# Rotary half turns of layer 2: from permutation matmuls on TensorE to signed multiplies on VectorE

## The chip, the core and the metric

The kernel runs on one core of one Trainium2 chip. A core has TensorE (PE in the profile; PEld is its loading of weights), VectorE (DVE), ScalarE (ACT) and GpSimd (POOL), each with an instruction queue of its own, worked off in order, and SyncE (SP), which issues DMAs. On-chip memory is SBUF (128 partitions) and PSUM, eight banks into which TensorE writes. Engines wait for each other by semaphores. The metric is the device time of one execution in microseconds (us).

## The reference, cut to what matters

Two transformer layers run one after the other over 256 tokens of width 1024, all in float32. The first has block attention (MoBA), a linear recurrence (RWKV) and a mixture of small experts (PEER). The second has sparse attention (NSA) and latent attention (MLA) side by side, and a gated feed-forward. The change concerns the rotary embedding of the second layer alone:

```python
def rope(x, pos):
    dim = x.shape[-1]
    half = dim // 2
    inv = ROPE_THETA_2 ** (-jnp.arange(half, dtype=jnp.float32) * 2.0 / dim)
    ang = pos[:, None] * inv[None, :]
    cos = jnp.cos(ang)[None, :, None, :]
    sin = jnp.sin(ang)[None, :, None, :]
    xf = x.astype(jnp.float32)
    x1, x2 = xf[..., :half], xf[..., half:]
    return jnp.concatenate([x1 * cos - x2 * sin, x1 * sin + x2 * cos], axis=-1).astype(x.dtype)
```

NSA rotates 14 head rows of width 128: eight queries, two keys for selection, two for the window (all normalised first) and two that are compressed later (not normalised). MLA rotates parts of width 64: one key part that all heads share, and eight query parts, which lie two to a row tile.

## The kernel before, in words

**Layout.** Activations lie transposed: features on the 128 partitions, the 256 tokens along the free axis. The scratch of a layer is one tensor, `arena`, so the trace calls most operands `arena`. `F2` in it holds 22 row tiles of 128x256: rows 0 to 11 are the normalised NSA heads, 12 and 13 the compressed ones, 16 to 20 the latents of MLA, 21 its shared key part. A rotation needs x*cos + turn(x)*sin, where turn swaps the two halves of a head across partitions and negates one of them.

**The projection `w_in2`.** Its 37 weight tiles (128 output features each) are loaded through a ring of six slots (`wring`). The first 32 are multiplied in split precision: ScalarE casts a tile to its upper part (`whi`, three slots, line 490), another engine subtracts that from the tile to get the lower part (`wlo`, line 495, `tile_lo`), and TensorE makes three matmuls for each of eight blocks (lines 501 to 503). The cast of tile k waits until TensorE is done with tile k-3, the subtraction waits for the cast, and TensorE waits for the subtraction before it starts a tile. The subtraction of tiles 13 to 31 is GpSimd's (`lo_phase` in the GpSimd block); before that it is VectorE's. The last five tiles (line 531) need no split.

**The norms and turns between the tiles.** TensorE's program has small pieces between the tiles, at places fixed by numbers: after tile 13 the sums of squares (line 2437), after tile 15 the norm factors given back to all partitions (line 2457), after tile 18 the turn `pe_nsa_turn` (line 2468: seven matmuls with the permutation `rot_nsa`, 128x512 columns each, into five banks), after tile 24 the sums for MLA's latents (`pe_rank_sums`, line 2445). VectorE runs `dve_nsa` beside it: squares (lines 2355, 2357), normalising multiplies that read PSUM (line 2364), the seven multiplies of the turned rows, read from PSUM, by the sine (line 2369), the cosine product (line 2373), the squares of the latents (line 2375, which waits until tile 20 has been copied out), the sum of both rotary parts (line 2377), the blocks for compression (line 2384), and the scaling of the latents (lines 2390, 2393), which releases MLA.

**MLA's up-projections and the attention.** `dve_mla` turns the shared key after the matmul of line 2697, which TensorE's list has behind the second key tile. The attention then runs 24 NSA jobs and eight MLA jobs in a pipeline of turns (`att_pe`, `att_dve`, `att_act`, `att_pool`). Of a job, TensorE makes scores, VectorE the maximum (line 832), ScalarE the exponential, VectorE the reciprocal (lines 847, 848), GpSimd the scaling of the probabilities (line 873, two instructions), TensorE the transposes (line 757) and the product with the values. Weight matmuls left over from the projection (line 2754) fill in between. At turns 4 and 7 TensorE makes the two matmuls of MLA's query turn (line 2703), and at turns 6, 8, 10 and 12 VectorE does the four steps of `turn_queries` (lines 2613 to 2620).

Of the kernel before, what the change touches and what calls it, by code (L numbers as in the profile page):

```python
# [12 lines left out]
ALU = mybir.AluOpType  # L13
# [89 lines left out]
CONST2 = [("rot_nsa", 128), ("rot_mla", 128), ("sum_all", 128), ("sum_rope", 64), ("give_all", 512),  # L103
# [17 lines left out]
def shape_constants():  # L121
# [31 lines left out]
    def table(width):  # L153
        half = width // 2
        inv = (np.float32(10000.0) ** (-np.arange(half, dtype=np.float32) * np.float32(2.0) / np.float32(width)))
        ang = np.arange(S, dtype=np.float32)[None, :] * inv.astype(np.float32)[:, None]
        ang = np.tile(ang, (128 // half, 1))
        return [np.cos(ang), np.sin(ang)]
# [3 lines left out]
    two = [rotation(128, 64), rotation(64, 32), sum_all, sum_rope, give_all,  # L162
# [27 lines left out]
def build_layer_pair(nc, a):  # L190

    with ExitStack() as ctx:
# [2077 lines left out]
        def pe_w_in2(pe):  # L2270
            first, ring0 = FIRST["w_in2"], RING0["w_in2"]

            for t in range(2, RAW2):
                pe.wait_ge(lo_ready, nth_split[first + t])
                if t >= 2 + BANKS:
                    pe.wait_ge(ring_free, ring0 + t - BANKS + 1)
                raw8(pe, bank[(ring0 + t) % BANKS], first + t).then_inc(tile_done, 1)
            pe.wait_ge(x_lo, XLO[3])
            ring_tiles_split(pe, "w_in2", RAW2, SUMS_AT)
            pe_nsa_sums(pe)  # L2280
            ring_tiles_split(pe, "w_in2", SUMS_AT, GIVE_AT)
            pe_nsa_give(pe)
            ring_tiles_split(pe, "w_in2", GIVE_AT, ROT_AT)
            pe_nsa_turn(pe)
            ring_tiles_split(pe, "w_in2", ROT_AT, RANK_AT)
            pe_rank_sums(pe)
            ring_tiles_split(pe, "w_in2", RANK_AT, SPLIT2)
            pe.wait_ge(xn_ready, 3 * KT)
            for k in range(SPLIT2, COUNT["w_in2"]):
                n, r = first + k, ring0 + k  # L2290
                pe.wait_ge(landed[n % SLOTS], count_at(n))
                pe.wait_ge(ring_free, r - BANKS + 1)
                matmul8_tokens(pe, bank[r % BANKS], n % SLOTS).then_inc(tile_done, 1)

        SUMS_AT, GIVE_AT, ROT_AT, RANK_AT = 14, 16, 19, 25
# [45 lines left out]
        n_qn, n_q = sem("n_qn"), sem("n_q")  # L2341
# [10 lines left out]
        def dve_nsa(dve, v):  # L2352
# [109 lines left out]

        def pe_nsa_turn(pe):
            pe.wait_ge(n_qn, 6)
            for g in range(7):
                if g >= 5:
                    pe.wait_ge(n_q, g - 4)
                pe.matmul(bank[3 + g % 5][:, :], c2["rot_nsa"], r2["F2"][:, 512 * g:512 * g + 512], start=True,
                          stop=True).then_inc(head_rot, 1)
# [87 lines left out]
        TURN_AHEAD = (4, 7)  # L2557
# [5 lines left out]
        def dve_mla(dve, v):  # L2563
# [8 lines left out]
            dve.wait_ge(head_rot, 9)  # L2572
            v.then(dve.tensor_tensor(ro[:, 4, :], bank[5][:, 0:S], c2["mla_sin"], ALU.mult))
# [36 lines left out]
            def turn_queries(step):  # L2610
                if step < 2:
                    dve.wait_ge(head_rot, 9 + step + 1)
                    dve.tensor_tensor(ro[:, 2 * step:2 * step + 2, :], two(2), over(c2["mla_sin"], 2), ALU.mult)\
                       .then_inc(n_q, 1)
                elif step == 2:
                    v.did(dve.tensor_tensor(qb[:, 8:12, :], qb[:, 8:12, :], over(c2["mla_cos"], 4), ALU.mult))
                elif step == 3:
                    dve.wait_ge(n_q, 9)
# [23 lines left out]
        def pe_mla(pe):  # L2642
# [52 lines left out]
            def turned_key():  # L2695
                pe.wait_ge(l_q, 1)
                pe.matmul(bank[5][:, 0:S], c2["rot_mla"], krr, start=True, stop=True).then_inc(head_rot, 1)

            def turned_queries(g):
                pe.wait_ge(l_q, 5)  # L2700
                if g:
                    pe.wait_ge(n_q, 8)
                pe.matmul(bank[2][:, :], c2["rot_mla"], r2["qb"][:, (8 + 2 * g) * S:(10 + 2 * g) * S],
                          start=True, stop=True).then_inc(head_rot, 1)

            for name, t in MIX:
# [4 lines left out]
                if (name, t) == ("uk", 1):  # L2711
                    turned_key()
                elif (name, t) == ("cmp_k", 5):
# [15 lines left out]
            def beside(t):  # L2729
# [5 lines left out]
                if t in TURN_AHEAD:  # L2735
                    turned_queries(TURN_AHEAD.index(t))
# [543 lines left out]
```

## Time and profile before

| what | value |
|---|---|
| device time, median of 3 runs | 1661.33 us (1660.74 to 1662.58) |
| span of the profiled execution | 1660.7 us |
| TensorE busy | 1620.8 us (98%) |
| VectorE busy | 1255.8 us (76%) |
| ScalarE busy | 823.8 us (50%) |
| GpSimd busy | 162.5 us (10%) |

The span is the time from the first to the last instruction of one execution; it is 0.6 us below the median of the timed runs. Busy time is what an engine's instructions cover together. The stretch of the projection in question lies from about 1208 us (GpSimd's first subtraction) to 1300 us (first up-projection of MLA), the attention from about 1350 us.

### The profile page before, as it was taken

How to read it: one execution, taken by the hardware profiler on the slowest of the kernel's cores; microseconds unless marked ns; L12 is line 12 of the kernel's file. 1: busy time of each engine (PE TensorE's matmuls, PEld its weight loads, DVE VectorE, ACT ScalarE, POOL GpSimd, SP SyncE). 2: the span in 40 equal slices, each digit the busy share in tenths (PEclk: the TensorE clock that was granted, in tenths of full speed). 3: DMA queues.
4: the chain of work that ended last, by engine and by line, in shares of the span. 5: the costliest groups of instructions: out<-in, count | busy, mean ns of one | idle time of the engine just before them, and what ended most of it. 6: DMA issues, size and time to landing. Idle time of an engine off the chain costs nothing.

```text
span 1660.7 us, 32559 instructions
## 1 busy us (share of the span) xinstructions
PE 1620.8 (98%) x11538; PEld 1430.8 (86%) x11538; DVE 1255.8 (76%) x2664; ACT 823.8 (50%) x1500; POOL 162.5 (10%) x134
## 2 busy tenths in 40 slices
PE   6999999999999999999999999999999999999998
PEld 4887988899988878888888888888889777999998
DVE  6885538759989988788888888888858256588887
ACT  3544111365469845555555555555744255544443
POOL 0020000017700000000000000000057014100000
PEclk9999999999999999999999999999999999999999
DMA  9742135855642288777777777777545651345553
GB/s 353 288 147 89 41 119 205 321 193 176 223 133 64 97 262 269 232 235 237 236 236 238 240 235 240 235 238 237 181 134 161 220 172 39 98 143 178 186 181 127
DMA packets 102625, 316.98 MB, mean 191 GB/s; under 512 B 11392, under 2 KB 21376, under 8 KB 102144
## 3 DMA queue, kind: packets, MB, share of 16 engines
q1 hardware_dynamic: 101664, 311.27, 56.3%
q10 hardware_dynamic: 864, 4.39, 0.7%
q8 instruction: 65, 1.06, 0.3%
q14 instruction: 32, 0.26, 0.1%
HBM read 309.71 MB, written 5.90 MB: 190 GB/s over the span
## 4 chain that ended last, share of the span: by engine, by line
PE 54%; DVE 15%; issue 14%; ACT 12%; DMA 2%; DVEq 1%; SPq 1%; POOL 0%; ACTq 0%
PE bank L501 9%; PE bank L502 9%; PE bank L503 9%; ACT whi L490 6%; DVE xn L2201 3%; PE bank L1301 3%; DVE Wlo L2184 2%; DVE arena L2190 2%; DVE wlo L495 2%; ACT arena L2031 2%; PE bank L2068 2%; PE bank L2070 2%; PE bank L2072 2%; PE bank L476 2%; PE bank L1587 2%
## 5 line engine op out<-in xcount | busy, mean ns | idle before, releaser
L490 ACT CAST whi<-wring 128x1024 fp32r<-128x1024 f32 x386 | 403.4, 1046 | 156.9 <-PE bank L503 84.7
L495 DVE TENSOR_TENSOR wlo<-wring,whi 128x1024 fp32r<-128x1024 f32 x341 | 415.3, 1223 | 52.2 <-ACT whi L490 42.8
L501 PE MATMUL bank<-xboth,whi 128*128 128x256 f32 x1032 | 296.9, 288 | 3.9 <-DVE wlo L495 2.2
L502 PE MATMUL bank<-xboth,whi 128*128 128x256 f32 x1032 | 291.9, 283 | 0.0
L503 PE MATMUL bank<-xboth,wlo 128*128 128x256 f32 x1032 | 291.9, 283 | 0.0
L501 PEld LDWEIGHTS bank<-xboth,whi 128*128 128x128 f32 x1032 | 197.8, 192 | 8.7 <-issue 3.8
L502 PEld LDWEIGHTS bank<-xboth,whi 128*128 128x128 f32 x1032 | 197.9, 192 | 0.7 <-issue 0.5
L503 PEld LDWEIGHTS bank<-xboth,wlo 128*128 128x128 f32 x1032 | 197.8, 192 | 0.0
L495 POOL TENSOR_TENSOR wlo<-wring,whi 128x1024 fp32r<-128x1024 f32 x45 | 114.9, 2560 | 811.7 <-ACT whi L490 811.6
L514 PE MATMUL bank<-xboth,whi 128*128 128x512 f32 x704 | 188.7, 390 | 0.0
L2068 PE MATMUL bank<-whi,Whi 128*128 128x512 f32 x512 | 159.7, 393 | 2.9 <-DVE Wlo L2184 2.9
L2070 PE MATMUL bank<-wlo,Whi 128*128 128x512 f32 x512 | 158.6, 391 | 0.0
L2072 PE MATMUL bank<-whi,Wlo 128*128 128x512 f32 x512 | 157.7, 389 | 0.0
L514 PEld LDWEIGHTS bank<-xboth,whi 128*128 128x128 f32 x704 | 132.5, 188 | 24.0
L2072 PEld LDWEIGHTS bank<-whi,Wlo 128*128 128x128 f32 x512 | 96.1, 188 | 21.0
L2070 PEld LDWEIGHTS bank<-wlo,Whi 128*128 128x128 f32 x512 | 96.1, 188 | 21.0
L2068 PEld LDWEIGHTS bank<-whi,Whi 128*128 128x128 f32 x512 | 95.1, 188 | 21.9 <-issue 3.1
L522 PEld LDWEIGHTS bank<-xboth,wlo 128*128 128x128 f32 x704 | 96.0, 190 | 6.9
L2139 ACT ACTIVATE arena<-arena 128x256 f32<-128x256 f32 x88 | 36.8, 418 | 128.0 <-DVE arena L2190 128.0
L522 PE MATMUL bank<-xboth,wlo 128*128 128x256 f32 x704 | 98.2, 282 | 0.0
L2193 DVE TENSOR_TENSOR arena<-arena 128x256 f32<-128x256 f32 x88 | 56.0, 636 | 52.4 <-ACT arena L2139 52.4
L2137 ACT COPY arena<-bank 128x256 f32<-128x256 f32 x88 | 32.9, 373 | 90.9 <-PE bank L514 90.9
(397 smaller groups left out, 2889.8 us busy)
## 6 DMA issues: line engine op xcount, KB each, us to landing
wring<-in_w SPq DMA_DIRECT2D x463, 512.0 KB, 3.5
arena<-in_ada SPq DMA_DIRECT2D x48, 512.0 KB, 7.4
xn<-in_ada SPq DMA_DIRECT2D x96, 256.0 KB, 2.7
h_spill<-arena SPq DMA_DIRECT2D x37, 128.0 KB, 1.7
arena<-h_spill SPq DMA_DIRECT2D x37, 128.0 KB, 3.9
wring<-in_w SPq DMA_DIRECT2D x6, 384.0 KB, 4.8
wring<-in_w SPq DMA_DIRECT2D x8, 256.0 KB, 3.3
arena<-in_const ACTq DMA_DIRECT2D x1, 1215.0 KB, 5.5
```

What stands on the lines that cost most here:

```text
L490: act.copy(whi[:, n % HSLOTS, :], wring[:, n % SLOTS, :]).then_inc(hi_ready, 1)
L495: eng.tensor_tensor(wlo[:, n % SLOTS, :], wring[:, n % SLOTS, :], whi[:, n % HSLOTS, :].bitcast(F32), ALU.subtract).then_inc(lo_ready, 1)
L501: pe.matmul(out, h, xh, start=start, stop=False, **kw)
L502: pe.matmul(out, h, xl, start=False, stop=False, **kw)
L503: return pe.matmul(out, l, xh, start=False, stop=stop, **kw)
L514: return pe.matmul(out, whi[:, n % HSLOTS, k * 128:k * 128 + 128], xboth[:, k, :, :], start=(k == 0), stop=(k == KT - 1))
L522: pe.matmul(out[:, 0:S], wlo[:, n % SLOTS, k * 128:k * 128 + 128], xhi[:, k, :], start=False, stop=False)
L1301: mm = pe.matmul(bank[r % BANKS][:, 0:S], blocks(tile % SLOTS, k), xn[:, k, :], start=(k == 0), stop=(k == KT - 1))
L2068: pe.matmul(tok_accs[b][f][:, :], Wh, h[:, f * 512:(f + 1) * 512], start=first, stop=False)
L2070: pe.matmul(tok_accs[b][f][:, :], Wh, l[:, f * 512:(f + 1) * 512], start=False, stop=False)
L2072: mm = pe.matmul(tok_accs[b][f][:, :], Wl, h[:, f * 512:(f + 1) * 512], start=False, stop=last)
L2193: dve.tensor_tensor(ge[:, b, :], ge[:, b, :], g, ALU.mult).then_inc(w_gated, 1)
```

## The change

The permutation matrices and every matmul with them go: seven in the projection, one for MLA's shared key, two for its queries. The sine table gets the sign of the turn: it holds the sine on the partitions of the first half of a head and minus the sine on those of the second. VectorE then multiplies one half's rows by the table's rows of the same half and writes the product on the partitions of the other half; both inputs of these multiplies lie in SBUF. For NSA these are two instructions on 64 partitions with 14x256 elements each, for MLA's key four on 32 partitions with 256, for its queries four on 32 partitions with 4x256, two at turn 6 and two at turn 8. They wait for the normalised rows instead of a matmul. `pe_rank_sums`, which waited until VectorE had read the turned banks, waits for the normalising multiplies.

```diff
-        return [np.cos(ang), np.sin(ang)]
+        return [np.cos(ang), np.where(p % width < half, 1.0, -1.0) * np.sin(ang)]
...
-            ring_tiles_split(pe, "w_in2", GIVE_AT, ROT_AT)
-            pe_nsa_turn(pe)
-            ring_tiles_split(pe, "w_in2", ROT_AT, RANK_AT)
+            ring_tiles_split(pe, "w_in2", GIVE_AT, RANK_AT)
...
+        thirtytwo = [slice(32 * i, 32 * i + 32) for i in range(4)]
+        nsa_swap = ((lo, hi), (hi, lo))
+        mla_swap = tuple((thirtytwo[i], thirtytwo[i ^ 1]) for i in range(4))
...
             dve.wait_ge(n_qn, 6)
-            for g in range(7):
-                dve.wait_ge(head_rot, 1 + g + 1)
-                ins = dve.tensor_tensor(ro14[:, 2 * g:2 * g + 2, :], bank[3 + g % 5][:, :].rearrange("p (m t) -> p m t", m=2),
-                                        over(c2["nsa_sin"], 2), ALU.mult)
-                ins.then_inc(n_q, 1)
-            dve.wait_ge(n_q, 7)
+            for dst, src in nsa_swap:
+                v.did(dve.tensor_tensor(ro14[dst, :, :], F2[src, 0:14, :], over(c2["nsa_sin"][src], 14), ALU.mult))
+            v.settle()
...
         def pe_rank_sums(pe):
-            pe.wait_ge(n_q, 7)
+            pe.wait_ge(n_qn, 6)
...
-            dve.wait_ge(head_rot, 9)
-            v.then(dve.tensor_tensor(ro[:, 4, :], bank[5][:, 0:S], c2["mla_sin"], ALU.mult))
+            for dst, src in mla_swap:
+                v.did(dve.tensor_tensor(ro[dst, 4, :], krr[src], c2["mla_sin"][src], ALU.mult))
+            v.settle()
...
                 if step < 2:
-                    dve.wait_ge(head_rot, 9 + step + 1)
-                    dve.tensor_tensor(ro[:, 2 * step:2 * step + 2, :], two(2), over(c2["mla_sin"], 2), ALU.mult)\
-                       .then_inc(n_q, 1)
+                    if step == 0:
+                        dve.wait_ge(l_q, 5)
+                    for dst, src in mla_swap[2 * step:2 * step + 2]:
+                        v.did(dve.tensor_tensor(ro[dst, 0:4, :], qb[src, 8:12, :], over(c2["mla_sin"][src], 4), ALU.mult))
...
-                if (name, t) == ("uk", 1):
-                    turned_key()
...
-                if t in TURN_AHEAD:
-                    turned_queries(TURN_AHEAD.index(t))
```

In the order of instructions on TensorE, at the end of the projection's tile 18 (lines 501 to 503 are the matmuls of a tile, line 2468 the turn), the kernel before has:

```order
L501 MATMUL bank<-xboth,whi 128x256
L502 MATMUL bank<-xboth,whi 128x256
L503 MATMUL bank<-xboth,wlo 128x256
L2468 MATMUL bank<-arena 128x512 x7
L501 MATMUL bank<-xboth,whi 128x256
L502 MATMUL bank<-xboth,whi 128x256
L503 MATMUL bank<-xboth,wlo 128x256
```

and the changed kernel at the same place:

```order
L501 MATMUL bank<-xboth,whi 128x256
L502 MATMUL bank<-xboth,whi 128x256
L503 MATMUL bank<-xboth,wlo 128x256
L501 MATMUL bank<-xboth,whi 128x256
L502 MATMUL bank<-xboth,whi 128x256
L503 MATMUL bank<-xboth,wlo 128x256
L501 MATMUL bank<-xboth,whi 128x256
```

The seven matmuls of the turn are gone, and the first matmul of tile 19 stands right behind the last one of tile 18.

In VectorE's order, the list of `dve_nsa` from the normalising multiplies on has before (line 2369 reads `bank`, PSUM):

```order
L2364 SCALAR_TENSOR_TENSOR arena<-arena,cols,bank 128x512 x6
L2369 TENSOR_TENSOR arena<-bank,arena 128x512 x7
L2373 TENSOR_TENSOR arena<-arena 128x3584
L2375 TENSOR_TENSOR arena<-arena 128x1280
L2377 TENSOR_TENSOR arena<-arena 128x3584
L2384 TENSOR_TENSOR arena<-arena,cols 128x16x15 x4
L2390 RECIPROCAL arena<-arena 128x512
L2393 SCALAR_TENSOR_TENSOR arena<-arena,cols 128x256 x5
L2384 TENSOR_TENSOR arena<-arena,cols 128x16x15 x4
```

and in the changed kernel:

```order
L2365 SCALAR_TENSOR_TENSOR arena<-arena,cols,bank 128x512 x6
L2369 TENSOR_TENSOR arena<-arena 64x3584 x2
L2371 TENSOR_TENSOR arena<-arena 128x3584
L2373 TENSOR_TENSOR arena<-arena 128x1280
L2375 TENSOR_TENSOR arena<-arena 128x3584
L2382 TENSOR_TENSOR arena<-arena,cols 128x16x15 x4
L2388 RECIPROCAL arena<-arena 128x512
L2391 SCALAR_TENSOR_TENSOR arena<-arena,cols 128x256 x5
L2382 TENSOR_TENSOR arena<-arena,cols 128x16x15 x4
```

In the place of seven multiplies of 512 columns that read PSUM stand two of 3584 columns on 64 partitions that read SBUF alone; the rest keeps its order, two line numbers lower.

In VectorE's order in the attention, at the first step of the query turn (line 832 is a job's maximum), before:

```order
L847 RECIPROCAL arena<-arena 128x2
L848 TENSOR_TENSOR arena<-arena 128x2
L2613 TENSOR_TENSOR arena<-bank,arena 128x512
L832 ISA arena<-bank,arena 128x128
L832 ISA arena 128x1
L832 ISA arena<-bank,arena 128x256
L832 ISA arena 128x1
L836 TENSOR_SCALAR arena<-arena 128x2
```

and in the changed kernel:

```order
L847 RECIPROCAL arena<-arena 128x2
L848 TENSOR_TENSOR arena<-arena 128x2
L2605 TENSOR_TENSOR arena<-arena 32x1024 x2
L832 ISA arena<-bank,arena 128x128
L832 ISA arena 128x1
L832 ISA arena<-bank,arena 128x256
L832 ISA arena 128x1
L836 TENSOR_SCALAR arena<-arena 128x2
```

One multiply of 512 columns from PSUM has become two of 1024 columns on 32 partitions from SBUF; the second step changes in the same way.

## Rows read from the trace of the kernel before

**Rows 1.** The page, busy time of each engine, and the granted clock by slices.

```profile
PE 1620.8 (98%) x11538; PEld 1430.8 (86%) x11538; DVE 1255.8 (76%) x2664; ACT 823.8 (50%) x1500; POOL 162.5 (10%) x134
...
PEclk9999999999999999999999999999999999999999
```

**Rows 2.** Busy time by windows: stretch us, PE, PEld, DVE, ACT, POOL, clock, DMA.

```profile
1227.70:1259.90 32.20, 32.20 (x232) 28.82 (x232) 20.98 (x15) 11.97 (x17) 20.48 (x8) 1.00 0.41 131
...
1600.00:1661.00 61.00, 56.20 (x467) 55.83 (x465) 48.47 (x88) 23.24 (x31) 0.00 (x0) 1.00 0.44 145
```

**Rows 3.** TensorE's timeline: start us, us, instructions [idle before <-releaser].

```profile
1236.46 6.17 PE L2468 MATMUL bank<-arena 128*128 128x512 f32 x14
1242.07 0.68 PE L501 MATMUL bank<-xboth,whi 128*128 128x256 f32 x1
```

**Rows 4.** The chain that ended last: start us, us, what.

```profile
1300.07 1.73 PE bank L2655 x8
...
1304.29 0.43 PE bank L2697 x2
...
1365.91 0.86 PE bank L2703 x2
```

**Rows 5.** VectorE's timeline over projection and MLA's start, columns as in rows 3.

```profile
1225.87 4.04 DVE L2364 SCALAR_TENSOR_TENSOR arena<-arena,cols,bank 128x512 f32<-128x512 f32 x6 [4.45 <-PE bank L2457]
1237.59 1.48 DVE L2369 TENSOR_TENSOR arena<-bank,arena 128x512 f32<-128x512 f32 x2 [7.68 <-PE bank L2468]
...
1243.40 3.89 DVE L2373 TENSOR_TENSOR arena<-arena 128x3584 f32<-128x3584 f32 x1
1249.83 3.52 DVE L2375 TENSOR_TENSOR arena<-arena 128x1280 f32<-128x1280 f32 x1 [2.54 <-ACT arena L2308]
1253.27 6.09 DVE L2377 TENSOR_TENSOR arena<-arena 128x3584 f32<-128x3584 f32 x1
...
1304.76 0.42 DVE L2573 TENSOR_TENSOR arena<-bank,arena 128x256 f32<-128x256 f32 x1 [21.82 <-PE bank L2697]
```

**Rows 6.** GpSimd's timeline in the projection, three windows.

```profile
1237.84 2.37 POOL L495 TENSOR_TENSOR wlo<-wring,whi 128x1024 fp32r<-128x1024 f32 x1 [0.49 <-ACT whi L490]
1246.72 5.28 POOL L495 TENSOR_TENSOR wlo<-wring,whi 128x1024 fp32r<-128x1024 f32 x2 [6.51 <-ACT whi L490]
...
1249.60 2.40 POOL L495 TENSOR_TENSOR wlo<-wring,whi 128x1024 fp32r<-128x1024 f32 x1
...
1252.47 3.13 POOL L495 TENSOR_TENSOR wlo<-wring,whi 128x1024 fp32r<-128x1024 f32 x1 [0.48 <-ACT whi L490]
```

**Rows 7.** GpSimd's line 495, whole run: duration ns min/median/max, starts.

```profile
L495 POOL TENSOR_TENSOR wlo<-wring,whi x45: 2365/2403/6029, 369.6 to 1274.8; 128x1024 fp32r<-128x1024 f32 x45
```

**Rows 8.** ScalarE's timeline in the projection.

```profile
1251.35 1.05 ACT L490 CAST whi<-wring 128x1024 fp32r<-128x1024 f32 x1 [1.56 <-PE bank L503]
...
1254.23 1.05 ACT L490 CAST whi<-wring 128x1024 fp32r<-128x1024 f32 x1 [1.56 <-PE bank L503]
```

**Rows 9.** VectorE's timeline in the attention.

```profile
1370.68 0.68 DVE L2613 TENSOR_TENSOR arena<-bank,arena 128x512 f32<-128x512 f32 x1
...
1375.18 0.68 DVE L2613 TENSOR_TENSOR arena<-bank,arena 128x512 f32<-128x512 f32 x1
...
1384.81 1.23 DVE L2620 TENSOR_TENSOR arena<-arena 128x1024 f32<-128x1024 f32 x1
```

**Rows 10.** GpSimd's timeline in the attention.

```profile
1370.86 0.84 POOL L873 TENSOR_SCALAR arena<-arena 128x128 f32<-128x128 f32 x2 [2.03 <-DVE arena L848]
...
1375.35 0.83 POOL L873 TENSOR_SCALAR arena<-arena 128x128 f32<-128x128 f32 x2 [1.68 <-DVE arena L848]
...
1384.99 1.75 POOL L873 TENSOR_SCALAR arena<-arena 128x128 f32<-128x128 f32 x2 [1.59 <-DVE arena L848]
```

**Rows 11.** TensorE's timeline in the attention, transposes of two jobs.

```profile
1372.11 0.49 PE L757 MATMUL bank<-keep,arena 128*128 128x128 f32 x3
...
1377.23 0.49 PE L757 MATMUL bank<-keep,arena 128*128 128x128 f32 x3
```

More of the change, by code:

```diff
@@ L102 @@
 SELECT1 = [("sum_pair", 64), ("give_pair", 256)]
-CONST2 = [("rot_nsa", 128), ("rot_mla", 128), ("sum_all", 128), ("sum_rope", 64), ("give_all", 512),
+CONST2 = [("sum_all", 128), ("sum_rope", 64), ("give_all", 512),
           ("nsa_cos", 256), ("nsa_sin", 256),
@@ L157, in table @@
         ang = np.tile(ang, (128 // half, 1))
-        return [np.cos(ang), np.sin(ang)]
+        return [np.cos(ang), np.where(p % width < half, 1.0, -1.0) * np.sin(ang)]
     t = np.arange(S).reshape(TT, 128).T[:, :, None]
     seen = (np.arange(NCMP) * CS + CB - 1)[None, None, :] <= t
-    two = [rotation(128, 64), rotation(64, 32), sum_all, sum_rope, give_all,
+    two = [sum_all, sum_rope, give_all,
            *table(128), *table(64), causal, np.where(seen, 0, NEG).reshape(128, -1), seen.any(-1),
@@ L2293, in pe_w_in2 @@
                 matmul8_tokens(pe, bank[r % BANKS], n % SLOTS).then_inc(tile_done, 1)
-        SUMS_AT, GIVE_AT, ROT_AT, RANK_AT = 14, 16, 19, 25
+        SUMS_AT, GIVE_AT, RANK_AT = 14, 16, 25
         raw_bank2 = lambda t: bank[5 + t] if t < 2 else ring_bank("w_in2", t)
@@ L2339, in build_layer_pair @@
         RAW_SCALED2 = RAW1 if 1 in RAWNORMS else 0
-        n_qn, n_q = sem("n_qn"), sem("n_q")
+        n_qn = sem("n_qn")
+        thirtytwo = [slice(32 * i, 32 * i + 32) for i in range(4)]
+        nsa_swap = ((lo, hi), (hi, lo))
+        mla_swap = tuple((thirtytwo[i], thirtytwo[i ^ 1]) for i in range(4))
         cm_x, cm_hs, cm_t, cm_ts, cm_o0, cm_kn, cm_kt, cm_kc, cm_rt = (sem(f"cm_{x}") for x in
@@ L2461, in pe_nsa_give @@
                     mm.then_inc(head_given, 1)
[L2463 to L2469, printed above, removed]
         def pe_compress(pe, i, name, t):
@@ L2556, in build_layer_pair @@
         TURN_QUERIES = (6, 8, 10, 12)
-        TURN_AHEAD = (4, 7)
         WO_UPPER, WO_LOWER = (11, 14, 17), (16, 19, 22)
@@ L2611, in turn_queries @@
                 if step < 2:
-                    dve.wait_ge(head_rot, 9 + step + 1)
-                    dve.tensor_tensor(ro[:, 2 * step:2 * step + 2, :], two(2), over(c2["mla_sin"], 2), ALU.mult)\
-                       .then_inc(n_q, 1)
+                    if step == 0:
+                        dve.wait_ge(l_q, 5)
+                    for dst, src in mla_swap[2 * step:2 * step + 2]:
+                        v.did(dve.tensor_tensor(ro[dst, 0:4, :], qb[src, 8:12, :], over(c2["mla_sin"][src], 4), ALU.mult))
                 elif step == 2:
+                    v.settle()
                     v.did(dve.tensor_tensor(qb[:, 8:12, :], qb[:, 8:12, :], over(c2["mla_cos"], 4), ALU.mult))
                 elif step == 3:
-                    dve.wait_ge(n_q, 9)
                     v.settle()
@@ L2693, in up @@
                 dict(uk=uk, uq=uq, uv=uv)[name](slot_of(n), bank[r % BANKS]).then_inc(tile_done, 1)
[L2695 to L2704, printed above, removed]
             for name, t in MIX:
@@ L2710, in pe_mla @@
                     pe_compress(pe, name == "cmp_v", name, t)
-                if (name, t) == ("uk", 1):
-                    turned_key()
-                elif (name, t) == ("cmp_k", 5):
+                if (name, t) == ("cmp_k", 5):
                     sums(1, 8)
```

## The prediction

> **What bounds the kernel now.** I read the page first: TensorE is busy for 98% of the span at the full granted clock [rows 1]. The windows then give the stretch of the change: from 1227.7 to 1259.9 us TensorE has no idle time at all, while GpSimd is busy for 20.5 and VectorE for 21.0 of 32.2 us [rows 2]. On this alone, work taken off TensorE would come out of the time whole. So the other engines' timelines come next, for how near each is to becoming the bound once the gap of the turn is closed. What the reader is to see there is a pair: the same subtraction takes GpSimd 2.37 us while VectorE works from PSUM, and up to 6.03 us elsewhere [rows 6, 7]; the same multiply of 3584 columns takes VectorE 3.89 us while GpSimd has nothing to subtract until 1246.72, nearly its end, and 6.09 us while GpSimd has subtractions to do [rows 5, 6]. Last, the chain of waits says which of the removed matmuls lie on the path: the one for MLA's key and those for its queries do [rows 4].
>
> **What is removed.** The seven matmuls of the projection hold back the tiles from 1236.46 to about 1242.45 (the first matmul of tile 19 starts at 1242.07 and runs on beside the last of the turn, 0.68 us) [rows 3]: 6.0 us. MLA's key takes 0.43 us, and two for its queries 0.86 us each [rows 4]; the second of them has no row here, as it repeats the first. That is 6.0 + 0.43 + 1.72 = 8.15 us of TensorE. VectorE no longer waits: it lay idle for 7.68 us before its first turned rows [rows 5], and for 21.82 us before the turned key.
>
> **What is added: first the rule of the rows.** The squares of the latents (1280 columns) began at 1249.83 and took 3.52 us; GpSimd's subtraction had begun at 1249.60 and ended at 1252.00, and the squares ended 1.35 us after that [rows 5, 6], about what 1280 columns take at the rate of 3584 in 3.89 us. The next subtraction, begun at 1252.47, ended at 1255.60 after 3.13 us instead of 2.40, and the sum of 3584 columns, begun at 1253.27, ended 3.76 us after that. So a VectorE instruction with both inputs in SBUF and a subtraction on GpSimd run one after the other, whichever came first, and in turns when both have more to do. The longest subtraction, 6.03 us [rows 7], is one that sat out those 3.7 us and then took its own 2.4. Multiplies that read one input from PSUM, as line 2369, left the subtraction beside them at 2.37 us [rows 5, 6].
>
> The Trainium skill states this in "SBUF — State Buffer", section "Who interferes with whom": a VectorE instruction with two SBUF inputs and a GpSimd instruction that reads SBUF share a read interface, and the second one to issue blocks until the first is done. The rows above agree, 3.76 us after the grant against 3.89 us alone. The rule speaks against this change, as its multiplies trade a PSUM input for an SBUF one; by a sum without it the projection would save its 6.0 us.
>
> **The projection, step by step.** The normalising multiplies end at 1229.91 [rows 5], and the first half's multiply starts at once. Two pair lengths follow from the rows: a 3584-column instruction and a subtraction together, 6.03 us [rows 7]; the squares and a subtraction, 1252.00 to 1255.60, 3.60 us [rows 6]. Casts come one tile of 2.88 us apart [rows 8], so GpSimd always finds a cast ready in what follows. Subtractions 13 to 18 are done. Then:
> - first half's multiply and subtraction 19: to 1236.0. TensorE, done with tile 18 at 1236.46, goes on without a wait.
> - second half's multiply and subtraction 20: to 1242.0. TensorE has been ready since 1239.3 and waits 2.7 us, with everything else on its queue behind the tile.
> - cosine product and subtraction 21: to 1248.0, a wait of 3.1 us.
> - squares and subtraction 22: to 1251.6, a wait of 0.7 us (tile 20's copy, which the squares need, is there by about 1246.5: the tile's end at 1244.9, a cast and a copy).
> - sum of both parts and subtraction 23: to 1257.7, a wait of 3.1 us.
>
> From there VectorE's instructions are short (240 columns, 0.25 us at the rate above), GpSimd needs about 2.65 us a tile against TensorE's 2.88, and TensorE waits no more. Before, tile 23 starts at 1242.45 + 4 x 2.88 = 1254.0, which fits the cast that its predecessor's end releases at 1254.23 [rows 8]. So the projection gets 1257.7 - 1254.0 = 3.7 us longer instead of 6.0 us shorter. Where an error could lie: handing over between two engines is counted inside the pairs; 0.05 us more or less at ten hand-overs is 0.5 us.
>
> **MLA's start.** TensorE loses 0.43 us there. VectorE gets four multiplies on 32 partitions; line 2573 with 256 columns took 0.42 us, so at most 1.7 us for one of 0.42. Its 21.82 us of idle time hide them; all of its work up to there was done at 1282.9, before TensorE began MLA at 1300.07 [rows 4, 5]. With the projection 3.7 us later on TensorE and about as much on VectorE, that cover stays. Without it, the cost would be 1.3 us.
>
> **The attention.** Steps 0 and 1 of the query turn cost VectorE one multiply from PSUM each, 0.68 us. Each becomes two of 1024 columns from SBUF, 1.23 us apiece by line 2620 [rows 9]. Behind them in VectorE's queue are the maxima of a later job; beside them GpSimd scales the probabilities that TensorE waits for. At line 2620 that pair of instructions took 1.75 us instead of 0.83 [rows 10], 0.92 us more. With two multiplies, GpSimd waits 0.92, does its first part (0.41), waits 1.07 for the second multiply (1024 columns at 3.76 us per 3584), and does the rest (0.41): 2.81 us, 1.98 more than now. TensorE's slack there is what passes between the end of the scaling and the transposes: 1371.70 to 1372.11 at the first step, 0.41 us, and 1376.18 to 1377.23, 1.05 us, at the second [rows 10, 11]. So TensorE waits about 1.6 and 0.95 us, against 1.72 us of matmuls gone: 0.8 us longer. Bounds: no collision at all, 1.72 us shorter; both scalings late without any slack, 3.96 - 1.72 = 2.2 us longer.
>
> **The sum.** 3.7 - 0.43 + 0.8 = 4.1 us, from the profiled execution's 1660.7 us to 1664.8. The median of the timed runs stands 0.6 above the span, so 1665.4 us, 0.25% slower. Behind the attention nothing changes, and the constants that the ScalarE queue loads get smaller by two matrices, at a place where nothing waits.
>
> What the trace does not show is a multiply on 64 partitions that reads one half and writes the other. The nearest row for its length is line 2373 with the same columns on 128 partitions, 3.89 us; I take that, as time here goes with columns. From below, it might leave GpSimd alone altogether (rival 1); from above, two such halves one after the other without a turn for GpSimd make 7.5 us of waiting for one subtraction, which by the same steps gives 1.1 us longer in the projection if the cosine product follows too (rival 3), and 3.4 us if it does not.
>
> **Rivals.**
> 1. *The half-row multiplies don't collide.* If 64 or 32 partitions, or the crossing of halves, go another way than rows 5 show, subtractions 19 to 21 come in time. The cosine product, now earlier and beside subtraction 21, then still collides with 22, the squares with 23, the sum with 24; by the same pairs tile 24 starts 1.0 us earlier than before. With 0.43 and 1.72 us it is 3.15 us shorter: 1658.2. For it: no such instruction has run beside GpSimd in this trace. Against it: even a multiply of 240 columns in line 2384 takes turns there.
> 2. *The matmuls come out whole, on the other side of zero.* Its place is the subtraction of tile 20: if that is ready by 1239.3, nothing of the above happens. It needs the long rows of GpSimd and VectorE to have another cause than each other, one that this change does not bring forward. Then 8.15 us go: 1653.2. For it: TensorE without a gap in the window [rows 2]. Against it: the long durations are, within 0.1 us, what the other engine had left plus what the work takes alone, at three hand-overs [rows 5 to 7].
> 3. *VectorE keeps going.* If the three long multiplies run without a turn for GpSimd, TensorE waits 7.1 us once, at tile 19, and the projection ends 1.1 us later; with the 0.43 and an attention where the same happens (GpSimd 2.2 us late at a step, 0.8 us longer): 1662.8. Against it: GpSimd came between two VectorE instructions at each chance in rows 5 and 6.
> 4. *The clock falls in TensorE's new gaps.* Four waits of 0.7 to 3.1 us within 20 us; at 1.2 instead of 2.4 GHz every microsecond of matmuls costs one more, so 3 us spent there give 1668.4. Against it: in the last 61 us TensorE idles for 4.8 us and the granted clock stays at 1.00 [rows 2].
>
> **How the numbers follow.** The forecast has a chance of 0.66; its own range is 1664.0 to 1667.0. Rival 1 has 0.12, rival 2 0.08, rival 3 0.09, rival 4 0.05. About 0.2% (3.3 us) is what a measurement can tell from no change, so 1658.0 and 1664.65 are the borders. Of the forecast's 0.66 about 0.54 lie above the upper one and 0.12 within; rival 4 adds 0.05 above. Half of rival 1 and all of rival 2 fall below the lower one, 0.14; the other half of rival 1 and rival 3 within. So faster 0.14, same 0.27, slower 0.59. The range leaves out rival 2 and most of rival 4 and takes in the rest, 1657.5 to 1668.0.
>
> **What would show it.** Right: GpSimd's subtractions 20, 21 and 23 in the new trace at about 6 us each from about 1236 on; VectorE's half-row multiplies at 3.9 us (the first) and 6.1 us (the second); TensorE waiting for GpSimd's line 495 in the projection, some 9.7 us in four waits, where it waits for nothing now; GpSimd's scaling at 2.8 us at two jobs of the attention; the new line of MLA's key not waited for. Wrong: subtractions at 2.4 us beside the half-row multiplies, or no wait on TensorE between tiles 18 and 24.

## The result, and the profile after

The changed kernel takes 1668.28 us (median of 5 runs, 1666.24 to 1669.43) against 1662.1 us for the kernel before (5 runs beside it, 1660.74 to 1662.78): a ratio of 1.0039, 95% interval 1.0028 to 1.0049, so 6.2 us slower where 4.1 us were forecast. The profiled execution's span is 1665.1 us, its own time 1666.98, which is 1.3 us below the median of the five. One timed run of all that follow, the sixth of the kernel with dummies ahead of tiles 20, 21 and 23, was a slow one (2006.77 us at a mean granted clock of 0.75) and enters no median.

The page of the changed kernel, busy time by engine and the group of GpSimd's subtractions (busy us, mean ns of one, idle before):

```profile
PE 1617.2 (97%) x11518; PEld 1430.5 (86%) x11518; DVE 1269.9 (76%) x2664; ACT 823.5 (49%) x1500; POOL 175.2 (11%) x134
...
L495 POOL TENSOR_TENSOR wlo<-wring,whi 128x1024 fp32r<-128x1024 f32 x45 | 123.7, 2755 | 807.3 <-ACT whi L490 807.3
```

TensorE has 20 matmuls (the trace has two for each of the program's ten) and 3.6 us of work less than in [rows 1]; the matmuls taken out were 8.15 us, and what runs longer in their place is shown below. GpSimd has the same 134 instructions and 12.7 us more in them. So something that GpSimd shares got dearer.

To see where, the trace is cut at three instructions that both kernels have: the first normalising multiply (1225.87 in [rows 5]), the squares of MLA's keys, and a subtraction of VectorE's behind the attention. The last two in VectorE's timeline before:

```profile
1310.37 2.29 DVE L2578 TENSOR_TENSOR arena<-arena 128x2048 f32<-128x2048 f32 x1 [4.26 <-ACT arena L2767]
...
1436.76 1.22 DVE L495 TENSOR_TENSOR wlo<-wring,whi 128x1024 fp32r<-128x1024 f32 x1 [1.11 <-ACT whi L490]
```

VectorE's timeline after (start us, us, instructions, idle before and what ended it):

```profile
1225.07 4.04 DVE L2365 SCALAR_TENSOR_TENSOR arena<-arena,cols,bank 128x512 f32<-128x512 f32 x6 [4.45 <-PE bank L2455]
1229.14 9.91 DVE L2369 TENSOR_TENSOR arena<-arena 64x3584 f32<-64x3584 f32 x2
1239.09 5.92 DVE L2371 TENSOR_TENSOR arena<-arena 128x3584 f32<-128x3584 f32 x1
1247.38 3.56 DVE L2373 TENSOR_TENSOR arena<-arena 128x1280 f32<-128x1280 f32 x1 [2.38 <-ACT arena L2306]
1250.86 6.09 DVE L2375 TENSOR_TENSOR arena<-arena 128x3584 f32<-128x3584 f32 x1
...
1285.21 1.76 DVE L2562 TENSOR_TENSOR arena<-arena 32x256 f32<-32x256 f32 x4
...
1313.68 2.29 DVE L2568 TENSOR_TENSOR arena<-arena 128x2048 f32<-128x2048 f32 x1 [25.80 <-ACT arena L2743]
...
1441.06 1.23 DVE L495 TENSOR_TENSOR wlo<-wring,whi 128x1024 fp32r<-128x1024 f32 x1 [1.11 <-ACT whi L490]
```

From the first mark to the second it is 88.61 us instead of 84.50 (projection and MLA's start, 4.11 longer), from the second to the third 127.38 instead of 126.39 (attention, 0.99 longer). Up to the first mark this execution happened to be 0.80 us ahead; up to the end hardly anything is added. These differences are used for every experiment, since the starts of the traces scatter by some 3 us (first mark from 1225.07 to 1227.83) whatever the edit.

GpSimd's timeline after, the subtractions of tiles 19 to 24:

```profile
1231.28 4.03 POOL L495 TENSOR_TENSOR wlo<-wring,whi 128x1024 fp32r<-128x1024 f32 x1 [3.73 <-ACT whi L490]
...
1235.26 6.00 POOL L495 TENSOR_TENSOR wlo<-wring,whi 128x1024 fp32r<-128x1024 f32 x1
...
1241.22 6.01 POOL L495 TENSOR_TENSOR wlo<-wring,whi 128x1024 fp32r<-128x1024 f32 x1
...
1247.20 2.39 POOL L495 TENSOR_TENSOR wlo<-wring,whi 128x1024 fp32r<-128x1024 f32 x1
...
1249.56 3.65 POOL L495 TENSOR_TENSOR wlo<-wring,whi 128x1024 fp32r<-128x1024 f32 x1
...
1253.16 6.00 POOL L495 TENSOR_TENSOR wlo<-wring,whi 128x1024 fp32r<-128x1024 f32 x1
```

The reader is to see the pairs of [rows 6, 7] again: each subtraction beside a multiply of 3584 columns lasts 6.0 us, the one beside the squares 3.65, the one alone 2.39. TensorE's waits between 1200 and 1450 us (us in total, times, longest):

```profile
PE bank L501 <- POOL wlo L495: 6.8, 3, 2.8
PE bank L757 <- POOL arena L873: 2.7, 3, 1.5
```

Before, the first did not exist there and the second was 0.4 us. TensorE's timeline at these waits:

```profile
1241.31 0.38 PE L501 MATMUL bank<-xboth,whi 128*128 128x256 f32 x1 [2.61 <-POOL wlo L495]
...
1242.47 0.41 PE L501 MATMUL bank<-xboth,whi 128*128 128x256 f32 x1
1242.68 0.41 PE L502 MATMUL bank<-xboth,whi 128*128 128x256 f32 x1
...
1247.29 0.38 PE L501 MATMUL bank<-xboth,whi 128*128 128x256 f32 x1 [1.34 <-POOL wlo L495]
...
1259.21 0.58 PE L501 MATMUL bank<-xboth,whi 128*128 128x256 f32 x1 [2.81 <-POOL wlo L495]
...
1262.76 0.28 PE L501 MATMUL bank<-xboth,whi 128*128 128x256 f32 x1
1262.88 0.28 PE L502 MATMUL bank<-xboth,whi 128*128 128x256 f32 x1
...
1263.48 0.81 PE L2443 MATMUL bank<-arena,keep 128*128 128x256 f32 x3
```

The matmuls after the first and the last wait start 0.21 us apart (1242.47, 1242.68), later again 0.12 (1262.76, 1262.88). The windows say why (stretch us, PE, PEld, DVE, ACT, POOL, then the granted clock, 1.00 being 2.4 GHz and 0.50 being 1.2 GHz):

```profile
1242.00:1244.00 2.00, 2.00 (x12) 2.00 (x11) 2.00 (x1) 0.00 (x0) 2.00 (x1) 0.50 0.00 0
1244.00:1246.00 2.00, 1.94 (x12) 1.74 (x11) 1.01 (x1) 0.00 (x0) 2.00 (x1) 0.72 0.00 0
...
1260.00:1262.00 2.00, 2.00 (x12) 2.00 (x11) 2.00 (x2) 0.00 (x0) 2.00 (x2) 0.50 0.00 0
```

So the waits also brought the low clock, twice, for some 3 us each.

### The profile page after: what moved, and what is told of

The parts are those of the page before. It is cut to its first block, busy times and chain, and to the rows that moved or that the text cites. A ratio compares the mean times of both kernels' runs of the same rounds, so it can differ in the third digit from the quotient of the medians.

```text
span 1665.1 us, 32516 instructions
## 1 busy us (share of the span) xinstructions
PE 1617.2 (97%) x11518; PEld 1430.5 (86%) x11518; DVE 1269.9 (76%) x2664; ACT 823.5 (49%) x1500; POOL 175.2 (11%) x134
## 4 chain that ended last, share of the span: by engine, by line
PE 51%; issue 15%; DVE 15%; ACT 12%; POOL 3%; DMA 2%; DVEq 1%; SPq 1%; ACTq 0%; POOLq 0%
PE bank L501 8%; PE bank L502 8%; PE bank L503 8%; ACT whi L490 6%; DVE xn L2201 3%; PE bank L1301 3%; DVE Wlo L2184 2%; DVE arena L2190 2%; DVE wlo L495 2%; POOL wlo L495 2%; ACT arena L2031 2%; PE bank L2068 2%; PE bank L2070 2%; PE bank L2072 2%; PE bank L476 2%
## 5 line engine op out<-in xcount | busy, mean ns | idle before, releaser
L495 POOL TENSOR_TENSOR wlo<-wring,whi 128x1024 fp32r<-128x1024 f32 x45 | 123.7, 2755 | 807.3 <-ACT whi L490 807.3
```

Of the source, the lines that this page charges most:

```text
L495: eng.tensor_tensor(wlo[:, n % SLOTS, :], wring[:, n % SLOTS, :], whi[:, n % HSLOTS, :].bitcast(F32), ALU.subtract).then_inc(lo_ready, 1)
```

## The experiments

Two theories to begin with. *Turns:* VectorE's multiplies with both inputs in SBUF and GpSimd's instructions run in turns, and that is the whole loss. *Clock:* a good part of it is TensorE's lower clock after the waits. With each group of runs the kernel before was timed again on the same chip, and the ratios are against those times.

**The changed kernel once more**, without an edit.

> The changed kernel once more, to fix the size of the change on one chip with the parts below. The traces so far differ by 4.4 us in span and the medians by 6.2 us. If the effect is the one seen in the trace (turn-taking on VectorE and GpSimd in the projection, 1.1 us in the attention, the lowered clock), it is 4.4 to 6.5 us slower than before; a run-to-run effect of another chip would show as under 3 us.

1668.48 us (1667.05 to 1671.53, 5 runs) against 1662.72 (21 runs): ratio 1.0035, 1.0021 to 1.0049. The waits are nearly the same (7.0 us in 3 instead of 6.8), but the clock fell only once. Its windows:

```profile
1242.00:1248.00 6.00, 3.93 (x22) 3.93 (x22) 5.77 (x1) 0.87 (x2) 6.00 (x2) 0.72 0.33 91
...
1260.00:1266.00 6.00, 4.03 (x29) 3.93 (x30) 6.00 (x3) 1.36 (x3) 6.00 (x3) 1.00 0.31 87
```

First to second mark: 87.32 us, 2.82 over before instead of 4.11. Same order and 1.29 us less, and the difference is tile 24 at full clock: here it takes 2.97 us (1261.97 to 1264.94) where it took 4.27 (1259.21 to 1263.48).

**NSA's half of the change alone, and MLA's alone**, each put into the kernel before:

```diff
-            ring_tiles_split(pe, "w_in2", GIVE_AT, ROT_AT)
-            pe_nsa_turn(pe)
-            ring_tiles_split(pe, "w_in2", ROT_AT, RANK_AT)
+            ring_tiles_split(pe, "w_in2", GIVE_AT, RANK_AT)
...
+            for dst, src in ((lo, hi), (hi, lo)):
+                v.did(dve.tensor_tensor(ro14[dst, :, :], F2[src, 0:14, :], over(c2["nsa_sin"][src], 14), ALU.mult))
```

```diff
-            dve.wait_ge(head_rot, 9)
-            v.then(dve.tensor_tensor(ro[:, 4, :], bank[5][:, 0:S], c2["mla_sin"], ALU.mult))
+            for dst, src in mla_swap:
+                v.did(dve.tensor_tensor(ro[dst, 4, :], krr[src], c2["mla_sin"][src], ALU.mult))
...
+                    for dst, src in mla_swap[2 * step:2 * step + 2]:
+                        v.did(dve.tensor_tensor(ro[dst, 0:4, :], qb[src, 8:12, :], over(c2["mla_sin"][src], 4), ALU.mult))
```

> The NSA part alone (no matmuls for the projection's turn, multiplies from SBUF there; MLA keeps its matmuls). Turn-taking: the projection gets some 4.5 us longer as in the whole change without the key's 0.43, so 4 to 6 us slower than before, with GpSimd's subtractions at 6 us. Rival (the loss comes from the MLA part, and the projection gains its matmuls): about 6 us faster than before.

> The MLA part alone (NSA keeps its matmuls). Turn-taking: minus 0.43 us for the key's matmul, minus 1.72 for the queries' two, plus about 2.7 us of TensorE waiting for GpSimd's scaling at two jobs, so 0 to 1 us slower than before. Rival (these waits lie beside other work): 2 us faster.

NSA alone: 1667.61 us, ratio 1.0033 (1.0024 to 1.0042, 11 runs). MLA alone: 1663.25 us, ratio 1.0 (0.9991 to 1.0009, 11 runs). TensorE's waits for GpSimd that are new, in the first and in the second (0.4 us of the second stood there before):

```profile
PE bank L502 <- POOL wlo L496: 6.9, 3, 2.8
```

```profile
PE bank L758 <- POOL arena L874: 2.7, 3, 1.5
```

NSA's half adds 3.23 us between the first two marks (with the key's matmul still in) and nothing in the attention (126.41); MLA's takes 0.45 there and adds 1.00 in the attention. Together 3.78, what the second trace of the changed kernel shows (2.82 + 1.00). The parts add up, and nearly all of the loss is NSA's.

**NSA's tables read from PSUM.** If turns are the cause, one input from PSUM ends them, with the same instructions on VectorE. ScalarE copies cosine and sine into bank 7 behind tile 15:

```diff
+                    act.copy(bank[7][:, :], r2["const2"][:, C2_AT["nsa_cos"]:C2_AT["nsa_cos"] + 2 * S]).then_inc(n_tab, 1)
...
-                v.did(dve.tensor_tensor(ro14[dst, :, :], F2[src, 0:14, :], over(c2["nsa_sin"][src], 14), ALU.mult))
+                v.did(dve.tensor_tensor(ro14[dst, :, :], F2[src, 0:14, :], over(nsa_tab["nsa_sin"][src], 14), ALU.mult))
```

The cosine product takes its table from there too.

> The changed kernel with NSA's cosine and sine tables copied to a PSUM bank by ScalarE, so that the two half-row multiplies and the cosine product keep their place, length and rows, but have one input in PSUM. Turn-taking on two SBUF inputs: VectorE runs them in 3.9 us each, GpSimd's subtractions 19 to 22 take 2.4 us, TensorE does not wait between tiles 18 and 25, and the projection is 6.0 us shorter than before: 1662.7 - 6.0 - 0.4 + 1.0 = about 1657.3. Rival (the crossing of halves or VectorE's longer list is what costs): as the changed kernel, 1668.

1657.67 us (8 runs, 1656.42 to 1659.55) against 1662.21: ratio 0.9975, 0.9965 to 0.9986, as expected. Its VectorE and a subtraction of GpSimd's beside it:

```profile
1230.40 7.80 DVE L2375 TENSOR_TENSOR arena<-arena,bank 64x3584 f32<-64x3584 f32 x2
1238.23 3.89 DVE L2377 TENSOR_TENSOR arena<-arena,bank 128x3584 f32<-128x3584 f32 x1
```

```profile
1235.40 2.42 POOL L495 TENSOR_TENSOR wlo<-wring,whi 128x1024 fp32r<-128x1024 f32 x1 [0.48 <-ACT whi L490]
```

and its first two marks:

```profile
1226.32 4.04 DVE L2370 SCALAR_TENSOR_TENSOR arena<-arena,cols,bank 128x512 f32<-128x512 f32 x6 [4.45 <-PE bank L2461]
...
1304.38 2.29 DVE L2574 TENSOR_TENSOR arena<-arena 128x2048 f32<-128x2048 f32 x1 [24.27 <-ACT arena L2749]
```

The two half-row multiplies take 7.80 instead of 9.91 us, the subtraction 2.42 instead of 6.00, and TensorE waits for no subtraction. From the first to the second mark it is 78.06 us, 6.44 shorter than before: the seven matmuls' 6.0 and the key's 0.43 come out whole. That one operand's place turns +4.11 into -6.44 shows the turns. It is what the Trainium skill states in "SBUF — State Buffer", section "Who interferes with whom", of two SBUF inputs, now seen in one kernel with and without the collision.

**MLA's tables read from PSUM**, in the query turn, by a copy into bank 2 at turn 2; NSA's part as in the changed kernel:

```diff
+                    act.copy(bank[2][:, :], r2["const2"][:, C2_AT["mla_cos"]:C2_AT["mla_cos"] + 2 * S]).then_inc(q_tab, 1)
...
-                        v.did(dve.tensor_tensor(ro[dst, 0:4, :], qb[src, 8:12, :], over(c2["mla_sin"][src], 4), ALU.mult))
+                        v.did(dve.tensor_tensor(ro[dst, 0:4, :], qb[src, 8:12, :], over(mla_tab["mla_sin"][src], 4), ALU.mult))
```

> The changed kernel with MLA's tables in PSUM bank 2 for the query turn alone. Turn-taking: GpSimd's scaling goes back from 2.8 to 0.8 us at the two jobs and from 1.5 to 0.6 at the third, TensorE waits less by 2.5 to 3 us, so 2.5 to 3 us faster than the changed kernel: about 1665.5. Rival (VectorE's own length, 2.4 instead of 0.7 us, delays the maxima): within 0.5 us of the changed kernel.

1668.2 us (6 runs, 1665.42 to 1668.64), ratio 1.0032 (1.002 to 1.0044): a miss. The attention got 1.5 us shorter than in the changed kernel (125.86 us), not the 2.5 to 3 expected, and in this trace the projection, with two falls of the clock at other tiles, was 0.75 us longer. Its VectorE, and its TensorE, at the first of the two pieces:

```profile
1375.46 2.45 DVE L2608 TENSOR_TENSOR arena<-arena,bank 32x1024 f32<-32x1024 f32 x2
```

```profile
1379.78 0.39 PE L760 MATMUL bank<-keep,arena 128*15 128x128 f32 x2 [0.55 <-POOL arena L873]
```

GpSimd's scaling beside the first piece is back at 0.84 us, but TensorE still waits, here 0.55 us and after the second piece 0.54. The reading, which is the rival of the expectation: the piece itself, 2.45 us, holds up the maxima behind it in VectorE's queue, and the next scaling starts late. The last experiment tests it.

**Both.** The two edits together.

> Both tables in PSUM. Turn-taking: the matmuls come out nearly whole, 8.15 us and 0.3 more at the cosine product of the queries: about 1654.3, 0.5% faster than before. Rival: what is gained in one place is lost in the other, over 1657.

1656.52 us (1655.43 to 1657.85), ratio 0.9966 (0.9952 to 0.998). The marks give -6.43 and -0.52, what the two edits gave apart. It is 2.2 us above the 1654.3 hoped for: by the marks 1.5 us of that lie in the attention, at the same waits as in the kernel before this one (0.55 and 0.55 us).

**The turn put off.** Instead of tables in PSUM, the twelve normalised heads are turned once GpSimd's last subtraction is done, from SBUF (the two that are compressed stay in place); MLA as in the last kernel:

```diff
+            dve.wait_ge(ring_free, ring0 + 14)
+            turn14(12, 14, latent_squares)
...
+            dve.wait_ge(lo_ready, nth_split[FIRST["w_in2"] + SPLIT2 - 1])
+            turn14(0, 12)
```

> The changed kernel with the turn of the 12 normalised heads moved behind GpSimd's last subtraction, into VectorE's idle time before MLA, from SBUF as it is; only the two heads for compression are turned in the projection. MLA's query tables in PSUM as in x4. Turn-taking: no subtraction is made to wait by a long multiply (only by the squares), so as x5: about 1654. Rival (length or crossing of the multiplies): also about 1654, but then x3 does not gain. If the moved 13 us of multiplies come too late for MLA, slower than x5 by what they are late.

1656.35 us (1654.35 to 1656.45), ratio 0.9961 (0.9948 to 0.9975); first to second mark -6.44, as with the tables in PSUM, and -0.20 in the attention. That is 2.3 us above the 1654 expected, but as near to the kernel with both tables (1656.52) as was expected. GpSimd's last subtraction ends at 1271.76; behind it VectorE has:

```profile
1273.13 6.74 DVE L2372 TENSOR_TENSOR arena<-arena 64x3072 f32<-64x3072 f32 x2
```

The same multiplies from SBUF cost nothing where GpSimd has nothing to do. So it is not the multiply that is dear, but its company.

**Dummy matmuls against the low clock.** Ten products with the identity (twenty matmuls in the trace, 2.40 us) each ahead of tiles 20, 21 and 24 of the changed kernel:

```diff
+            for k in (20, 21, 24):
+                pe_warm(pe, 7, 10)
+                ring_tiles_split(pe, "w_in2", k, {20: 21, 21: 24, 24: 25}[k])
```

> The changed kernel with ten matmuls of 128 columns of no use (2.15 us each time) ahead of tiles 20, 21 and 24, where TensorE waits 2.6, 1.3 and 2.8 us for GpSimd. If TensorE's gaps lower the granted clock and that costs what tile 24 took too long (4.27 us instead of 2.88), the clock stays at 1.00 from 1236 to 1264 us and the time is 0.5 to 1.4 us below the changed kernel's. If the lower clock costs nothing that is not hidden by the wait, it is the same within 0.3 us; if the gaps are not what lowers the clock, it falls to half all the same.

1672.95 us (1670.7 to 1673.51), ratio 1.0058 (1.0044 to 1.0072), where up to 1.4 us less than the changed kernel was expected: a miss by aim. The clock stayed at 1.00 up to 1254; tile 20 then came through in time, the squares took their turn where the prediction had them, and the long wait moved to tile 23, where no dummy stood. Its TensorE and its window there:

```profile
1257.70 0.39 PE L501 MATMUL bank<-xboth,whi 128*128 128x256 f32 x1 [2.83 <-POOL wlo L495]
```

```profile
1254.00:1260.00 6.00, 3.17 (x20) 2.96 (x19) 5.97 (x3) 2.71 (x3) 6.00 (x2) 0.85 0.37 112
```

The dummies ahead of tile 24 came on top.

**The dummies ahead of tiles 20, 21 and 23.**

```diff
-            for k in (20, 21, 24):
+            for k in (20, 21, 23):
```

> As x6_warm, but the matmuls of no use stand ahead of tiles 20, 21 and 23, since in x6 the squares came in time for their turn and the long wait was at tile 23, not 24. If the lowered clock is what moved that wait and what makes the changed kernel's runs scatter, the clock stays at 1.00 from 1236 to 1266 us, the waits stand where the forecast put them (20, 21, 23, a short one at 22), the way from the normalising multiplies to the squares of the MLA keys is 3.3 us longer than before (84.5 us), as forecast, and the five times lie closer together than the changed kernel's 3.2 and 4.5 us. If the scatter has another cause, they don't.

1667.67 us (5 runs, 1666.67 to 1668.82), ratio 1.0034 (1.002 to 1.0047). The five lie within 2.2 us, those of the changed kernel within 3.2 and 4.5, as expected. Its waits, and its clock:

```profile
PE bank L501 <- POOL wlo L495: 2.1, 4, 0.6
```

```profile
1242.00:1254.00 12.00, 10.55 (x86) 9.96 (x85) 11.12 (x3) 2.64 (x4) 12.00 (x4) 1.00 0.28 88
1254.00:1266.00 12.00, 11.40 (x90) 11.00 (x89) 11.96 (x5) 5.60 (x8) 12.00 (x5) 1.00 0.40 121
```

With the clock held, the four waits stand at tiles 20 to 23, as the prediction listed them (the dummies fill most of three), and first to second mark is 3.34 us over before; the prediction's terms were 3.7 - 0.43 = 3.27. So the steps came out to 0.1 us for a TensorE at full clock. What the clock does to them is read from four traces of the same code in the projection and this one with dummies, each with the key's matmul taken off:

| trace | clock fell after the wait at | first to second mark, against before |
|---|---|---|
| changed kernel | tiles 20, 24 | +4.11 |
| changed kernel again | tile 20 | +2.82 |
| NSA alone | tile 20 | +2.80 (3.23 - 0.43) |
| MLA's tables in PSUM | tiles 20, 23 | +4.86 |
| dummies at 20, 21, 23 | nowhere | +3.34 |

The fall at tile 20 costs nothing: that tile is slow inside time that tile 21 waits anyway, and its late copy can send the squares behind a subtraction, which saves 0.5 us (second row against fifth). The fall at the last wait costs 1.3 (first row against second) to 1.5 us (fourth against fifth, which have the same order of turns), since behind it nothing waits. Whether it comes differs between runs of one code.

The runs without a trace bear this out, as the mean granted clock of each is on record. In the traces it is 0.999 where the clock did not fall in the projection, 0.998 where it fell once and 0.997 where it fell twice. In the second five runs of the changed kernel, 0.998 goes with 1667.05 to 1668.48 us (three runs), 0.996 with 1670.29 and 1671.53. So part of the scatter of the changed kernel is the clock.

**The query turn in smaller pieces**: both tables in PSUM, and one multiply a turn instead of two.

```diff
-        TURN_QUERIES = (6, 8, 10, 12)
+        TURN_QUERIES = (5, 6, 8, 9, 11, 12)
```

> As x5_both_psum, with the four multiplies of the query turn one a turn (turns 5, 6, 8, 9; cosine at 11, sum at 12) instead of two and two. If what was left of TensorE's waits in x5's attention (1.4 us) comes from VectorE's 2.45 us in one piece, the waits fall under 0.8 us and the attention gets 0.5 to 1 us shorter than x5's 125.9 us (from the squares of the keys to the first subtraction of the last layer stage): about 1655.5. If it comes from GpSimd, the same as x5.

1654.46 us (1653.04 to 1656.58) against 1662.07: ratio 0.9954, 0.994 to 0.9968, the fastest here and faster than both kernels; 1655.5 was expected. TensorE's waits for GpSimd in the attention are back at 0.4 us, as before the change. A piece of its VectorE, and GpSimd's scaling beside it:

```profile
1361.08 1.21 DVE L2614 TENSOR_TENSOR arena<-arena,bank 32x1024 f32<-32x1024 f32 x1
```

```profile
1361.14 0.83 POOL L873 TENSOR_SCALAR arena<-arena 128x128 f32<-128x128 f32 x2 [0.83 <-DVE arena L848]
```

The attention takes 124.39 us, 2.00 less than before and 1.47 less than with the four multiplies two by two, where 0.5 to 1 was expected. So what was left of the waits there came from the length of VectorE's pieces. All that the matmuls cost, 6.0 + 0.43 + 1.72 us, is now out of the time: 8.4 us by the marks, 7.6 by the medians.

## Why the prediction was right, and where it fell short

- *The mechanism* was right: turns between VectorE and GpSimd, and TensorE waiting for line 495, are shown by the tables in PSUM and by the turn put off. Rival 1 (half rows don't collide) falls with 9.91 us against 7.80; rival 2 (matmuls come out whole) is what happens once the collision is gone, not before; rival 3 (VectorE keeps going) falls with GpSimd's turn between the two half-row multiplies.
- *The pairs* were right: forecast ends of subtractions 19 to 21 were 1236.0, 1242.0 and 1248.0; with the 0.80 us by which this trace runs ahead put back, they ended at 1236.1, 1242.1 and 1248.0. The unknown length of the half-row multiply, taken as 3.89 us, was 3.90 (half of 7.80).
- *The fourth and fifth step* came in another order, so that TensorE waited 6.8 us in three waits instead of the 9.7 in four that the prediction gave as its sign: tile 20 ran at the low clock, its copy was late, VectorE waited 2.38 us for it, and the sum's turn fell on tile 24 instead of 23. Tile 24 thus started 0.6 us earlier than forecast (1259.21 + 0.80 = 1260.0 against 1257.7 + 2.88 = 1260.6), but took 4.27 us instead of 2.88 (1259.21 to 1263.48). 1.39 - 0.6 is the 0.8 us by which the 4.11 exceeds the forecast 3.27.
- *MLA's key*: -0.43 forecast, -0.45 measured; its four multiplies took 1.76 us and were hidden, with 25.80 us of idle time behind them.
- *The attention*: +0.8 forecast, +0.99 and +1.00 measured. The scaling beside the query turn was to take 2.81 us and took 2.82 and 2.81; the waits were to be 1.6 and 0.95 and were 1.45 and 0.83. That the total is so near is in part luck: these waits are 0.3 us shorter than forecast, while TensorE's busy time between the marks fell by 1.29 us (124.03 to 122.74) and not by the 1.72 of the two matmuls; why is not shown. The rows:

```profile
1373.31 2.82 POOL L873 TENSOR_SCALAR arena<-arena 128x128 f32<-128x128 f32 x2 [2.03 <-DVE arena L848]
...
1378.62 2.81 POOL L873 TENSOR_SCALAR arena<-arena 128x128 f32<-128x128 f32 x2 [1.03 <-DVE arena L848]
```

```profile
1376.18 0.55 PE L757 MATMUL bank<-keep,arena 128*128 128x128 f32 x3 [1.45 <-POOL arena L873]
...
1381.49 0.55 PE L757 MATMUL bank<-keep,arena 128*128 128x128 f32 x3 [0.83 <-POOL arena L873]
```

- *The step that failed* is the sum, 3.7 - 0.43 + 0.8: it has nothing for TensorE's clock, which the prediction set aside as rival 4, "The clock falls in TensorE's new gaps", with a chance of 0.05. It was set up as another case, though its gaps were the forecast's own: it had to be a term on top of the 4.1, with its own range. The reason given against it, a clock of 1.00 over the last 61 us with 4.8 us idle, looked at no such gap: of that idle time 3.8 us lie behind the last matmul, which ends at 1657.18, and the rest is one gap of 0.98 us ahead of 1654.08. Nor can [rows 1] show a clock that never falls: a slice there is 41.5 us, and its digit 9 stands for 0.90 or more; the first slice has a mean of 0.96. The trace of before held the row that mattered elsewhere, near its start. Its TensorE timeline and two windows:

```profile
22.29 5.37 PE L1088 MATMUL bank<-wring,xn 128*128 128x512 f32 x8 [2.47 <-ACT xn L585]
29.64 3.70 PE L1088 MATMUL bank<-wring,xn 128*128 128x512 f32 x8 [1.99 <-ACT xn L585]
```

```profile
22.00:24.00 2.00, 1.71 (x3) 0.71 (x4) 1.62 (x2) 0.93 (x3) 0.00 (x0) 0.62 1.02 408
24.00:26.00 2.00, 2.00 (x4) 0.93 (x3) 1.93 (x4) 0.00 (x0) 0.00 (x0) 0.53 1.03 412
```

  One wait of 2.47 us, and the eight matmuls after it took 5.37 us, where the next eight took 3.70: 1.67 us more, near the 1.3 to 1.5 us that the last fall cost here. By the table above the clock was a term from -0.5 to +1.5 us here (+0.8 net in the trace of the result, where the last of its two falls cost 1.3), and with it the upper ends of both ranges would have stood 1.5 us higher. That rival 4's 1668.4 us is so near the measured 1668.28 is luck: it counted 3 us for the clock, and the trace shows 0.8.
- *The rest of the miss* of 2.9 us: 0.8 us is the kernel before, 1662.1 in the comparison where the first three runs gave 1661.33; 2.1 us is the change, 6.2 instead of 4.1. Of these the traces show up to 0.8 (clock, at the profiled execution) and 0.2 (attention). The other 1.1 lies outside what was summed: the two traces of the changed kernel put it 5.1 and 3.8 us over before between first and third mark, the medians 6.2 and 5.8. More falls of the clock in the untraced runs do not explain it: four of the five runs of the result have the mean granted clock of the traced one, 0.997, and with the dummies ahead of tiles 20, 21 and 23, where all five stand at 0.999 or 1.000, the median is still 1.2 us over what the marks give (5.6 against 4.4). The same holds in all ten series of runs without NSA's matmuls: the median stands 0.8 to 2.2 us above what the marks give. With MLA's half alone, which keeps them, it is 0.0 (0.53 against 0.55). This points to about 1 us that NSA's half costs outside the marks, which the prediction put at nothing. It is not shown: a single case lies within the noise, all marks of the kernel before come from one trace, and what precedes the first mark differs by up to 3 us between traces. Its cause stays open.
- *What tipped it:* the measured time lies 0.28 us above the range's upper end, 1668.0. Any one of the three, the clock (0.8), the base (0.8) or the cost outside the marks (1.1), is enough for that; the clock is the one whose mechanism is shown.

## What to carry to other kernels

Before work moves from TensorE to VectorE, look what runs beside it on GpSimd and where the operands lie: a multiply that read PSUM and now reads two SBUF inputs takes turns with GpSimd, and whoever waits for GpSimd pays. The cheap cure is one operand in PSUM (a table copied there once by an engine with time), or a moment in which GpSimd is idle, in pieces no longer than the slack of what queues behind. And a long new wait of TensorE (here 2.47 to 2.83 us, though not each time) is priced twice, as the wait and as slower matmuls behind it where nothing else waits; the trace of before is to be searched for the longest gap that has matmuls behind it, which the idle sum of a window does not show.

## What the runs showed of the hardware that was not expected

- The granted clock fell to 0.50 in a kernel in which TensorE is 97% busy, after single waits of 2.61 us (in all four traces without dummies that have that wait) and, in some of the traces, of 2.8 us; after waits of 1.34 to 1.57 us there, and of 1.99 us in the trace of before, it stayed at 1.00. Twenty small matmuls in such a gap (2.40 us) held it at 1.00.
- A multiply on 64 partitions that writes the other half takes as long as one on 128 (3.90 against 3.89 us for 3584 columns), and takes turns with GpSimd just as the latter does.
- With one input in PSUM neither the multiply (3.89 us) nor the subtraction beside it (2.42 us against 2.39 alone) got longer by more than 0.03 us.
